# The output projection of a two-layer streaming encoder step: tokens stationary instead of weights stationary

## The reference

```python
def layer(l, x):                      # x: 256 prompt rows, and 32 sample rows
    o, new = token_mix(rms_norm(x, ln_attn[l]), pos, cache, *weights[l])
    x = x + o
    return x + channel_mix(rms_norm(x, ln_ffn[l]), l, ...)

def token_mix(h, ...):
    ...                               # two attention groups, 512 + 512 columns
    o = jnp.concatenate([o_a, o_b], axis=-1)
    return jnp.einsum('btm,md->btd', o, w_o), new     # w_o: 1024 x 1024

def channel_mix(h, l, ...):           # layer 0: swiglu(h), inner width 2816
    ...                               # layer 1: router, top 2 of 8 experts
```

## Time and profile before

| | us |
|---|---|
| median of 3 runs | 1610.37 |
| lowest, highest | 1608.53, 1615.91 |
| span of the profiled execution | 1611.3 |
| TensorE busy (matmul) | 1511.3 |
| VectorE busy | 1024.3 |
| ScalarE busy | 813.2 |
| output projection, layer 0, first product to last eviction's start | 35.1 |
| output projection, layer 1, the same | 35.5 |

### The profile page before, as it was taken

One profiled execution on the slowest core, in us unless ns is written; L12 is line 12 of the kernel. 1 busy time (PEld: TensorE's weight loads), 2 busy tenths in 40 slices (PEclk: granted clock), 3 DMA queues, 4 the chain that ended last, 5 costly groups with the idle time before them and its releaser, 6 DMA issues.

```text
span 1611.3 us, 19980 instructions
## 1 busy us (share of the span) xinstructions
PE 1511.3 (94%) x7475; PEld 1224.1 (76%) x7475; DVE 1024.3 (64%) x1102; ACT 813.2 (50%) x914; POOL 24.5 (2%) x60
## 2 busy tenths in 40 slices
PE   6969889999989698889999999999999999999995
PEld 3448669999954486768888888888888888888884
DVE  2464244444334642638789698698796896986984
ACT  2233343433222333427667576576575775765762
POOL 2010000000000100000000000000000000000000
PEclk9975889999999758769999999899899999998996
DMA  6040054544300300619989898798798797987983
GB/s 232 26 139 1 1 183 139 174 158 158 125 29 27 140 0 1 208 44 337 317 298 327 294 349 319 263 349 319 283 367 306 282 321 289 364 316 265 358 302 131
DMA packets 173119, 344.15 MB, mean 214 GB/s; under 512 B 8320, under 2 KB 50016, under 8 KB 173072
## 3 DMA queue, kind: packets, MB, share of 16 engines
q1 hardware_dynamic: 171744, 341.16, 60.2%
q0 software_dynamic: 1264, 2.34, 0.4%
q10 hardware_dynamic: 64, 0.02, 0.0%
HBM read 341.61 MB, written 1.88 MB: 213 GB/s over the span
## 4 chain that ended last, share of the span: by engine, by line
PE 90%; DVE 5%; ACT 3%; issue 1%; DMA 0%; POOL 0%; SPq 0%; DVEq 0%; ACTq 0%
PE ps L1598 30%; PE ps L1627 16%; PE ps L1505 9%; PE ps L1563 6%; PE ps L1327 5%; PE ps L1521 4%; PE ps L1480 4%; PE ps L1429 3%; PE ps L1460 3%; PE ps L1571 2%; PE ps L1613 1%; PE ps L1441 1%; PE ps L1296 1%; PE ps L1340 1%; PE ps L1392 1%
## 5 line engine op out<-in xcount | busy, mean ns | idle before, releaser
L913 DVE TENSOR_TENSOR w_lo<-ring,w_hi 128x2048 fp32r<-128x2048 f32 (+1 forms) x326 | 687.9, 2125 | 187.2 <-ACT w_hi L647 185.6
L647 ACT ACTIVATE w_hi<-ring 128x2048 fp32r<-128x2048 f32 (+1 forms) x326 | 579.2, 1791 | 209.8 <-PE ps L1598 85.4
L1598 PE MATMUL ps<-w_hi,xg_hi 128*128 128x512 f32 (+1 forms) x768 | 289.8, 377 | 3.8 <-DVE xg_lo L1208 3.8
L1598 PE MATMUL ps<-w_lo,xg_hi 128*128 128x512 f32 (+1 forms) x768 | 286.7, 373 | 0.0
L1598 PE MATMUL ps<-w_hi,xg_lo 128*128 128x512 f32 (+1 forms) x768 | 286.1, 373 | 0.0
L1598 PEld LDWEIGHTS ps<-w_hi,xg_hi 128*128 128x128 f32 x768 | 145.2, 189 | 29.2 <-issue 3.9
L1598 PEld LDWEIGHTS ps<-w_lo,xg_hi 128*128 128x128 f32 x768 | 145.1, 189 | 26.1
L1598 PEld LDWEIGHTS ps<-w_hi,xg_lo 128*128 128x128 f32 x768 | 145.3, 189 | 24.8
L1627 PE MATMUL ps<-w_hi,am_hi 128*128 128x512 f32 x352 | 146.7, 417 | 0.2
L1627 PE MATMUL ps<-w_hi,am_lo 128*128 128x512 f32 x352 | 144.4, 410 | 0.0
L1627 PE MATMUL ps<-w_lo,am_hi 128*128 128x512 f32 x352 | 143.4, 407 | 0.0
(11 more groups left out here) (246 smaller groups left out, 1881.8 us busy)
## 6 DMA issues: line engine op xcount, KB each, us to landing
ring<-in_moe_w_gate SPq DMA_DIRECT2D x84, 1024.0 KB, 6.1
ring<-in_moe_w_up SPq DMA_DIRECT2D x82, 1024.0 KB, 6.3
ring<-in_moe_w_down SPq DMA_DIRECT2D x80, 1024.0 KB, 6.2
ring<-in_ffn_w_gate SPq DMA_DIRECT2D x11, 1024.0 KB, 5.5
ring<-in_ffn_w_up SPq DMA_DIRECT2D x11, 1024.0 KB, 5.4
ring<-in_ffn_w_down SPq DMA_DIRECT2D x10, 1024.0 KB, 5.1
ring<-in_w_in SPq DMA_DIRECT2D x8, 1024.0 KB, 8.0
ring<-in_w_o SPq DMA_DIRECT2D x8, 1024.0 KB, 5.2
```

Of the source, the lines that this page charges most:

```text
L647: A(hi[:, 0:size], src[:, 0:size], ACT.Copy).then_inc(hi_ready, 1)
L913: V.tensor_tensor(lo[:, 0:size], src[:, 0:size], hi[:, 0:size].bitcast(F32), ALU.subtract).then_inc(lo_ready, 1)
L1598: ins = mm_(ps[:, 2 * (1 - q) + m, 0:WIDTH[c]], (xg_hi, xg_lo)[xp][:, k, :], w[wp][:, k % 4, :], start=(k == 0 and n == 0), stop=(k == KD ...
```

## The change

The projection is turned round. The outer loop runs over the three token tiles. For a tile, 8 blocks of `hT` (128 x the tile's tokens) are the stationary side, in two passes over 512 output columns each, and `w_o` in the ring is the moving side. The sum in PSUM is rows of 1024 outputs, one pair of banks per tile (job `wr`), and VectorE adds it to `xres` at once. `yT`, its evictions, `turn_back` for the projection, and the jobs `wo` and `ty` go. ScalarE's second norm waits for its own tile's sum instead of for all. The three splits stand ahead of the norm on ScalarE, and ahead of one tile's addition each on VectorE. A slot of the ring is released during the last tile; the last one at the first transpose of the norm behind it (`last_of`).

```diff
@@ psum_plan
-        for d in range(KD + 1):
-            if d < KD:
-                jobs.append(("wo", l, d))
-            if d >= 1:
-                jobs.append(("ty", l, d - 1))
+        jobs += [("wr", l, t) for t in range(3)]
@@ ScalarE
-                        wait_out(act, ("ty", l, KD - 1))
+                        wait_out(act, ("wr", l, t))
...
-                for d in range(KD):
-                    wait_full(act, ("wo", l, d))
-                    if d >= 2:
-                        wait_full(act, ("ty", l, d - 2))
-                    free(A(yT[:, 0, d % 2, :], pair(("wo", l, d))[:, 0:TOK], ACT.Copy), ("wo", l, d))
-                    if d == 0:
-                        act.wait_ge(stored, 16 * 10 * (l + 1))
-                    if d in SPLIT_AT and l == 0:
-                        dense_hi_part(SPLIT_AT.index(d))
-                    elif d in SPLIT_AT:
-                        moe_hi_part(0, SPLIT_AT.index(d), first=True)
+                act.wait_ge(stored, 16 * 10 * (l + 1))
+                for i in range(3):
+                    if l == 0:
+                        dense_hi_part(i)
+                    else:
+                        moe_hi_part(0, i, first=True)
                 norm(l, 1)
@@ VectorE
-                for d in range(KD):
-                    add_rows(("ty", l, d), d)
-                    if l == 1 and d == 4:
+                for t in range(3):
+                    r, key = ROWS[t], ("wr", l, t)
+                    if l == 0:
+                        dense_lo_part(t)
+                    else:
+                        moe_lo_part(0, t, first=True)
+                    wait_full(dve, key)
+                    free(V.tensor_tensor(xres[0:r, t, :], xres[0:r, t, :], pair(key, r), ALU.add), key)
+                    if l == 1 and t == 1:
...
-                    if d in SPLIT_AT and l == 0:
-                        dense_lo_part(SPLIT_AT.index(d))
-                    elif d in SPLIT_AT:
-                        moe_lo_part(0, SPLIT_AT.index(d), first=True)
@@ TensorE
-            def turn(key, src, rows):
+            def turn(key, src, rows, last_of=None):
...
+                    if k == 0 and last_of:
+                        used_up(ins, last_of)
...
-                for d in range(KD + 1):
-                    if d < KD:
-                        key = ("wo", l, d)
-                        wait_room(pe, key)
+                for t in range(3):
+                    r, key = ROWS[t], ("wr", l, t)
+                    wait_room(pe, key)
+                    for c in range(2):
                         for k in range(KD):
-                            wk = ("wo", l, d // 4, k // 4)
+                            wk = ("wo", l, c, k // 4)
                             weights(wk)
-                            ins = mm_(pair(key)[:, 0:TOK], slot(wk, 4, 512)[:, k % 4, (d % 4) * P:(d % 4 + 1) * P], hT[:, k, :],
+                            ins = mm_(pair(key, r)[:, 512 * c:512 * c + 512], hT[:, k, TOFF[t]:TOFF[t] + r], slot(wk, 4, 512)[:, k % 4, :],
                                       start=(k == 0), stop=(k == KD - 1))
-                            if d % 4 == 3 and k == 3:
+                            if t == 2 and k % 4 == 3 and not (c == 1 and k == KD - 1):
                                 used_up(ins, wk)
-                        full(ins, key)
-                    if d >= 1:
-                        turn_back(("ty", l, d - 1), yT[:, 0, (d - 1) % 2, :], ("wo", l, d - 1),
-                                  last_of=("wo", l, d // 4 - 1, 1) if d % 4 == 0 else None)
+                    full(ins, key)
                 for t in range(3):
                     pe.wait_ge(xn_ready, norm_no(l, 1, t))
-                    turn(("hf", l, t), xn[:, t, :], ROWS[t])
+                    turn(("hf", l, t), xn[:, t, :], ROWS[t], ("wo", l, 1, 1) if t == 0 else None)
```

More of the change, by code:

```diff
@@ L472, in build @@
         SC_BANKS = (0, 4, 4)
-        SPLIT_AT = (2, 3, 5)
         DOWN_USED = 10
@@ L825, in down_out @@
                             wait_full(act, ("dn", c, h))
-                            wait_full(act, ("tz", 2 * h + 1) if c else ("ty", 0, KD - 1))
+                            if c:
+                                wait_full(act, ("tz", 2 * h + 1))
                             v = pair(("dn", c, h)).rearrange("p (f c) -> p f c", f=2)[:, :, 0:TOK]
```

## The result

The changed kernel takes 1628.14 us (median of 5 runs, 1624.92 to 1636.03), the kernel before 1610.37 beside it (5 runs, 1605.19 to 1616.54): ratio 1.0114, 95% interval 1.0079 to 1.0149. That is +17.8 us, where the forecast was +11.2 and its range ended at 1627. Slower was right; the size was not.

The account below looks back on a forecast made before the run. TensorE, busy 94% of the span with 90% of the chain, was taken as the bound. Two streams of +8.5 less tails of 3.1 and 2.7 gave +11.2 on 1610.4, so 1621.6; range 1614 to 1627.

Parts of the forecast that it names:

- The price of a tile: Output projections: each token tile, even with 32 tokens, costs 13.86, so 41.6 per layer against 31.5 before.
- The rival of the cheap wide product: Output projections: a 512-column instruction costs what a 288-column one does, -24.8 in all, 1585.6; chance 0.03.
- The stream: TensorE's products in both output projections, less the dropped transposes: 8.5 longer per layer, 17.0 in all.
- The clock's loss at the start (1.8 and 2.3) stays: Start of each output projection: time lost at the lower clock, 1.8 and 2.3, is the same after the change.
- The tails: Behind each projection's last product: early norms of tiles 0 and 1 save 3.1 in layer 0, 2.7 in layer 1.
- the short end, 9.4: Layer 0 behind the projection: with the upper clock, the first dense product starts 9.4 behind E, against 13.19 before.
- The splits and loads: Around the projection's end: three weight splits per layer and the ring's loads hide, priced at zero; third split fits by 0.1.
- The rival of the late split: Projection tails: slot 2's load takes 10 instead of 5.6, delaying the norms; +18.0, 1628.4; chance 0.09.
- The clock did not stay up: Rival at both tails: clock stays at 1.00, also speeding first dense products and router; +4.7, 1615.1; chance 0.12.
- the expert stage of the same length: Expert stage, outside the change: expected to keep its length in the changed profile, so nothing was added.
- some 3 either way, since the three times of before lie 7 apart: Whole kernel: scatter allowance on the forecast, part of its own range of 1617 to 1626.

Follow-up runs that it names:

- the four-strip kernel: Changed kernel with the 32-token tile first, its eight contraction blocks on four strips of 32 output partitions: 1607.42 against 1615.91 for the kernel before (0.9938).
- the second profile of the changed kernel: Changed kernel run again, nothing altered: 1631.9 against 1614.18 for the kernel before (1.0111); the profiled run took 1624.28.
- The experiment with the norms held back: Changed kernel, but ScalarE's squares of all three tiles wait for the last tile's add: 1626.49 against 1614.18 for the kernel before (1.0079).
- with 8 and with 16 products more: Changed kernel with 8 or 16 unread 128x224 products added before the dense network's fifth gate: 1.0038 and 1.0064 against the kernel before.
- Six places of the same change: Changed kernel with 0, 4, 8, 16, 24, 32 unread products before the fifth dense gate: 1.0111, 1.0091, 1.0038, 1.0064, 1.0072, 1.0147 against the kernel before.
- the same-chip steps of 5.3, 7.4 and 9.4: Changed kernel with added dense-network products, compared within one chip: 16 instead of 8 took 5.3 more, 24 instead of 8 took 7.4, 32 instead of 4 took 9.4.
- the flat shifts of the kernel before: Kernel before with 8, 16 or 24 products of 224 columns added in its dense network: 1.0008, 1.0013 and 1.0015 against the kernel before unpadded.
- the third set: Changed kernel, nothing altered, timed on another occasion: 1629.29 against 1610.7 for the kernel before (1.0111).

## Why the prediction was wrong, point by point

**The price of a tile was right.** 13.86 per tile was taken from the input projection; the adds stand 13.74 and 13.85 apart, for 32 tokens as for 128. The rival of the cheap wide product is dead: 13.8 / 32 = 0.43 per instruction of 512 columns. The Trainium skill ("TensorE: Matmul & The Clock Gate", section Back-to-back issue gap) would have 0.13; the trace does not agree, for these float32 operands.

**The stream came out 1.2 longer.** 9.34 + 8.90 = 18.2 for 17.0. The step "The clock's loss at the start (1.8 and 2.3) stays" failed in part. The windows of the changed kernel show it at the lower clock until about 193.7, 5.7 behind the start, where before it had left it at about 3.6:
```profile
193.00:194.00 1.00, 1.00 (x3) 0.42 (x2) 0.00 (x0) 0.00 (x0) 0.39 (x2) 0.65 0.00 0
194.00:195.00 1.00, 1.00 (x4) 0.49 (x3) 0.00 (x0) 0.00 (x0) 0.00 (x0) 1.00 0.00 0
```
44.42 - 3 x 13.86 = 2.8 was lost there in place of 1.8, and 44.36 - 41.6 = 2.8 in place of 2.3 in layer 1. The loss in layer 0 goes by the run: in the other two profiles of the same kernel it was 2.0 and 3.1. In the four-strip kernel the same start was low for 3.9 only.

**The tails were right in mechanism.** -2.65 lies inside the -2.4 to -3.8 given for layer 0, with every step in its place: `xn` of tile 0 written 2.1 behind E, the transposes 4.23 long, `hT_hi` at E + 6.4, and 4.15 from there to the first product. In layer 1 the router came at E + 7.61, not 7.0 to 7.25. The three scalings were taken as one run behind the third `xn`. In the trace the last two wait for transposes at the lower clock (start 692.25, E + 5.8) and end at E + 7.35. Together -4.9 for -5.8. In the second profile of the changed kernel the clock stayed at 1.00 over layer 0's transposes, and the dense network started at E + 9.32, near the short end, 9.4. Its last add and its first dense product:
```profile
230.70 1.21 DVE L1086 TENSOR_TENSOR xres<-xres,ps 32x1024 f32<-32x1024 f32 x1 [0.69 <-PE ps L1475]
...
240.02 0.58 PE L1497 MATMUL ps<-hT_hi,w_hi 128*128 128x288 f32 x1 [4.62 <-DVE hT_lo L1101]
```
The experiment with the norms held back gives the same from the other side: 3.6 of it is the early norms.

**The splits and loads hid, as priced.** The third split started at E - 5.07 (forecast E - 5.0), its load 5.2 behind its issue at 222.12. The rival of the late split did not occur; that its +18.0 equals the result is chance, since its place, the tails, shows nothing of it.

**The clock did not stay up.** The router's window has it at 0.60 and its products took 6.65 instead of 7.92, so part of that rival came true (1.3). The dense network paid about as much back: it ran at 0.50 until 248, 5.0 behind its start, where before it was up after 3, and that stage is 1.0 longer. ```profile
243.00:248.00 5.00, 5.00 (x21) 5.00 (x22) 0.00 (x0) 0.00 (x0) 0.00 (x0) 0.50 1.10 348
...
694.10:700.80 6.70, 6.61 (x48) 6.49 (x48) 5.35 (x5) 1.50 (x2) 0.00 (x0) 0.60 1.05 389
```
In other profiles the pauses behind E did leave the clock up, with the same instructions around them: in layer 0 in the changed kernel's second one, and in both layers with 8 and with 16 products more. With 8 more, the transposes of the norm in layer 1, and the router:
```profile
683.40:686.00 2.60, 2.57 (x24) 2.29 (x24) 2.53 (x5) 2.57 (x5) 0.00 (x0) 1.00 0.36 65
687.90:694.10 6.20, 6.18 (x48) 6.12 (x48) 5.37 (x4) 2.04 (x2) 0.00 (x0) 0.65 1.06 393
```
So that rival had its own price wrong: its pauses survived, but the router's products took 6.21 and not half of 7.92, because the clock fell while they ran.

**What failed: the stages outside the change, and the range.** The prediction held "the expert stage of the same length" and gave its sum "some 3 either way, since the three times of before lie 7 apart". The stages that the change rewrites came to +13.3, +11.2 and +13.5 in three profiles, for the forecast of 11.2. The other 5 or so (17.8 less about 13) lie in stages it does not touch, at the lower clock: +3.2 in the attention and +2.6 in the experts in the first profile. The prediction put these stages at nothing, because they run the same instructions; it had no term for the clock in them. With the changed stages alone the time would have been 1621.6 to 1623.9, inside the range. Six places of the same change, at most 3.6 apart in work, gave +5.0 to +20.1 with the mean +12.4, over two chips. Three times of before could not show that; by these six, a range should have been some 8 either way. The rival that named the clock looked at it only at the two tails, and only for a gain.

**What stays open.** Why the changed kernel runs more of its untouched stages at the lower clock is not shown. The stage windows and the clocks of the runs show that the clock is lower. Theory C, that the kernel's place decides it, has the same-chip steps of 5.3, 7.4 and 9.4 for it, the flat shifts of the kernel before against it, and the change of chip between the rows unresolved. The place alone doesn't fix which stage pays: the profiles of the one unaltered kernel differ by 3.3 in the experts and by 5.2 in all that stands ahead of the projection (182.8 in the third set's, 188.0 in the first), and the kernel before has such a step too (182.4 and 186.7). Nothing here lets one compute this cost ahead of time. The run that would decide is the changed kernel and its shifts, all six on one chip.

## What to carry over

Price a product by its moving columns times its instruction count: a tile with few stationary columns costs a full one, so before turning operands round, see what the ragged tile costs, and put it on strips that run side by side. Norms and splits that were queued behind a last reader are worth moving under the last tile's products. And where TensorE's clock goes up and down through untouched stages, don't read a change of a per cent or less from one profile each: time it in several sets on one chip, with small shifts of the same kernel beside it, and give its forecast a range as wide as these.

## What the hardware showed that was not expected

Float32 products of 32 stationary columns and 512 moving ones, aimed in turn at four strips of 32 output partitions, ran four at a time: four instructions in 0.43, against 0.43 for each one without strips (a product is two instructions). The Trainium skill ("TensorE: Matmul & The Clock Gate", section Measured speedup vs the span model) gives 2.38 times for three such tiles; the ratio seen here is 4.0, for four, at either clock.

The same 4100 products of the expert stage took 884.15, 886.47 or 889.75 of TensorE's busy time (8 products more, the second and the first profile of the changed kernel), with VectorE's and ScalarE's busy time within 1.5. So the granted clock of TensorE alone moves a stage that nobody touched by 3 to 6 us, and the last two of these figures are of one unaltered kernel.

The same pause of 2.2 ahead of the same transposes in layer 0 ended at a granted clock that stayed at 1.00 in one profile of the changed kernel (24 transposes in 2.58), and fell to 0.50 in another (4.23).
